# Byte classes modulo 256 of weights and rows in a two-layer hybrid block on one Trainium2 core

## What is computed

```python
a_b, a_c, a_u, q, k, v, r_g, r_u, d_v, d_g, gl = _split_cols(h @ w_in)
ys = (_short_conv(a_b, a_c, a_u, conv_a) @ w_a_out, y_b @ w_b_out,
      (jax.nn.gelu(r_g) * rec) @ w_c_out,
      _conformer_conv(d_v, d_g, conv_d, conv_d_b, ln_d_g, ln_d_b) @ w_d_out)
out = _merge(gl, ys, w_out)                      # sum of sigmoid gates times ys, @ w_out
x = x + gt1 * o
x = x + gt2 * _swiglu(_modulate(x, g_ffn[l], sh2, sc2), w_ffn_in[l], w_ffn_out[l])
```

## Time and profile before

| | |
|---|---|
| median of 3 runs | 1960.27 us (1960.24 to 1960.73) |
| the profiled execution | 1960.5 us |
| its span, first to last instruction | 1958.7 us |
| mean granted TensorE clock | 0.997 |
| TensorE busy | 1930.0 us, 11006 matmuls |
| VectorE, ScalarE, GpSimd busy | 1416.5, 908.0, 812.0 us |
| bytes read from HBM | 273.70 MB |

### The profile page before, as it was taken

One profiled execution on the slowest core, in us unless ns is written; L12 is line 12 of the kernel. 1 busy time (PEld: TensorE's weight loads), 2 busy tenths in 40 slices (PEclk: granted clock), 3 DMA queues, 4 the chain that ended last, 5 costly groups with the idle time before them and its releaser, 6 DMA issues.

```text
span 1958.7 us, 29316 instructions
## 1 busy us (share of the span) xinstructions
PE 1930.0 (99%) x11006; PEld 1671.1 (85%) x11006; DVE 1416.5 (72%) x2475; ACT 908.0 (46%) x1439; POOL 812.0 (41%) x353
## 2 busy tenths in 40 slices
PE   7999999999999999999999999999999999999998
PEld 5778888888888888887888888878899999999998
DVE  5896666677789868798885544689788787645455
ACT  5787544232223343345222223599854435565443
POOL 1002322344444444344344444301647886454432
PEclk9999999999999999999999999999999999999999
DMA  8222211222232235534455442322334554544543
GB/s 344 86 86 81 92 65 65 85 88 107 86 105 88 100 138 216 192 129 170 174 219 192 190 175 83 140 78 106 130 108 151 180 186 174 193 172 172 194 174 127
DMA packets 38701, 276.25 MB, mean 141 GB/s; under 512 B 4416, under 2 KB 4416, under 8 KB 6336
## 3 DMA queue, kind: packets, MB, share of 16 engines
q1 hardware_dynamic: 38592, 274.77, 38.2%
HBM read 273.70 MB, written 1.05 MB: 140 GB/s over the span
## 4 chain that ended last, share of the span: by engine, by line
PE 81%; DVE 13%; ACT 3%; issue 2%; DMA 0%; POOL 0%; SPq 0%; DVEq 0%; ACTq 0%; POOLq 0%
PE PS L592 80%; DVE PS L1545 3%; DVE TMP L1542 1%; DVE TMP L1545 1%; ACT WH L1023 1%; DVE TMP L1548 1%; PE PS L905 1%; DVE S L1545 1%; ACT PS L1023 1%; DVE PS L1542 1%; DVE SM L1991 1%; DVE HL L1545 0%; DVE TMP L1864 0%; DVE ZL L1542 0%; DVE WL L1542 0%
## 5 line engine op out<-in xcount | busy, mean ns | idle before, releaser
L535 POOL TENSOR_TENSOR WL<-RAW,WH 128x1024 fp32r<-128x1024 f32 (+1 forms) x337 | 802.8, 2400 | 1122.9 <-ACT WH L1023 1122.9
L1023 ACT ACTIVATE WH<-RAW 128x1024 fp32r<-128x1024 f32 (+1 forms) x416 | 414.4, 1043 | 606.0 <-PE PS L592 571.4
L592 PE MATMUL PS<-HH,WH 128*128 128x512 f32 (+2 forms) x1968 | 680.7, 346 | 7.3 <-POOL WL L535 3.2
L592 PE MATMUL PS<-HH,WL 128*128 128x512 f32 (+2 forms) x1968 | 667.5, 339 | 0.0
L592 PE MATMUL PS<-HL,WH 128*128 128x512 f32 (+2 forms) x1968 | 666.9, 340 | 0.3 <-DVE HL L1545 0.3
L592 PE MATMUL PS<-ZH,WH 128*128 128x512 f32 (+1 forms) x1312 | 442.1, 337 | 3.7 <-DVE HL L1542 2.9
L592 PE MATMUL PS<-ZH,WL 128*128 128x512 f32 (+1 forms) x1312 | 441.0, 336 | 0.0
L592 PE MATMUL PS<-ZL,WH 128*128 128x512 f32 (+1 forms) x1312 | 439.3, 337 | 0.3 <-POOL ZL L559 0.3
L592 PEld LDWEIGHTS PS<-HH,WH 128*128 128x128 f32 x1968 | 373.0, 190 | 55.8 <-issue 8.2
L592 PEld LDWEIGHTS PS<-HL,WH 128*128 128x128 f32 x1968 | 372.6, 190 | 44.0 <-issue 3.8
L592 PEld LDWEIGHTS PS<-HH,WL 128*128 128x128 f32 x1968 | 373.0, 190 | 41.3
(11 more groups left out here) (210 smaller groups left out, 1740.3 us busy)
## 6 DMA issues: line engine op xcount, KB each, us to landing
RAW<-in_stream SPq DMA_DIRECT2D x200, 1024.0 KB, 4.8
CD<-in_modw SPq DMA_DIRECT2D x22, 1024.0 KB, 7.1
G<-in_modw SPq DMA_DIRECT2D x22, 1024.0 KB, 6.9
RAW<-in_stream SPq DMA_DIRECT2D x8, 768.0 KB, 4.2
CD<-in_lruw SPq DMA_DIRECT2D x2, 2048.0 KB, 11.7
X<-in_xT SPq DMA_DIRECT2D x2, 1024.0 KB, 7.1
S<-in_modw SPq DMA_DIRECT2D x2, 1024.0 KB, 12.9
RAW<-in_modw SPq DMA_DIRECT2D x1, 1024.0 KB, 19.8
```

The source lines that it names most:

```text
L535: nc.gpsimd.tensor_tensor(WL[:, a:b], RAW[:, a:b], WH[:, a:b].bitcast(F32), ALU.subtract)\
L592: return nc.tensor.matmul(out, lhs, rhs, start=start, stop=stop)
L1023: return nc.scalar.activation(out, in_, f, **kw)
```

## The change

The second slot of WH, WL and RAW begins 32 words (128 bytes) later than the end of the first slab, by a new constant SLOT that replaces SLAB as the step between slots wherever these tensors are indexed (loads, splits, products, the home of one slab of the modulation's weights). The tensors change their order, with one 128-byte tensor in each gap, so that WH, WL, HH and HL begin at 0 modulo 256 in their first slot, the second slots of WH and WL at 128, and ZH and ZL at 128. RAW's first slot is at 128 and its second at 0. S and CD stay at 128, TMP and G go from 128 to 0, PADA from 0 to 128. All the tensors up to SM end 384 bytes later.

```diff
+SLOT = SLAB + 32
...
         MOD = sb("MOD", 2 * 48)
         X = sb("X", KC * NT)
-        WH = sb("WH", 2 * SLAB, F32R)
-        WL = sb("WL", 2 * SLAB, F32R)
+        WH = sb("WH", SLOT + SLAB, F32R)
+        SELB = sb("SELB", 32)
+        WL = sb("WL", SLOT + SLAB, F32R)
+        AMP = sb("AMP", 2 * 2 * KC)
+        HH = sb("HH", KC * UROW, F32R)
+        LC = sb("LC", 2 * 16)
+        HL = sb("HL", KC * UROW, F32R)
         ZH = sb("ZH", KC * NT, F32R)
         ZL = sb("ZL", KC * NT, F32R)
-        HH = sb("HH", KC * UROW, F32R)
-        AMP = sb("AMP", 2 * 2 * KC)
-        SELB = sb("SELB", 32)
-        LC = sb("LC", 2 * 16)
-        HL = sb("HL", KC * UROW, F32R)
         S, SR = sb_and_rounded("S", KC * NT)
         CD = sb("CD", KC * NT)
-        RAW = sb("RAW", 2 * SLAB)
+        RAW = sb("RAW", SLOT + SLAB)
...
-                a, b = s * SLAB + h * half, s * SLAB + (h + 1) * half
+                a, b = s * SLOT + h * half, s * SLOT + (h + 1) * half
...
-                a = s * SLAB + k * 2 * P + t * P
+                a = s * SLOT + k * 2 * P + t * P
...
-                        w0 = SLAB + k * 2 * P
+                        w0 = SLOT + k * 2 * P
```

More of the change, by code:

```diff
@@ L316, in build @@
         MOD_HOMES = [S[:, 0:SLAB], S[:, SLAB:2 * SLAB], CD[:, 0:SLAB], CD[:, SLAB:2 * SLAB],
-                     RAW[:, SLAB:2 * SLAB], TMP[:, 2 * NT:6 * NT], G[:, 0:SLAB], G[:, SLAB:2 * SLAB]]
+                     RAW[:, SLOT:SLOT + SLAB], TMP[:, 2 * NT:6 * NT], G[:, 0:SLAB], G[:, SLAB:2 * SLAB]]
         MOD_ORDER = [j + h * (MOD_FIRST // 2) for j in range(MOD_FIRST // 2) for h in range(2)]
@@ L459, in load @@
             def load(n, s, words=SLAB):
-                sp.dma_start(RAW[:, s * SLAB:s * SLAB + words], slab_of(stream, n)[:, 0:words]).then_inc(raw_loaded[s], 16)
+                sp.dma_start(RAW[:, s * SLOT:s * SLOT + words], slab_of(stream, n)[:, 0:words]).then_inc(raw_loaded[s], 16)
             def load_unit(w):
@@ L1028, in high @@
                 for h in halves:
-                    x = slice(s * SLAB + h * half, s * SLAB + (h + 1) * half)
+                    x = slice(s * SLOT + h * half, s * SLOT + (h + 1) * half)
                     fn(WH[:, x], RAW[:, x], ACT.Copy).then_inc(hi_done[s], 1)
@@ L1632, in low @@
                 dve.wait_ge(hi_done[s], 2 * m + 2)
-                x = slice(s * SLAB + half, s * SLAB + 2 * half)
+                x = slice(s * SLOT + half, s * SLOT + 2 * half)
                 tt(WL[:, x], RAW[:, x], WH[:, x].bitcast(F32), SUB).then_inc(lo_done[1][s], 1)
@@ L1810, in lows @@
                         dve.wait_ge(hi_done[s], 2 * m + (h + 1))
-                        x = slice(s * SLAB + h * HALF, s * SLAB + (h + 1) * HALF)
+                        x = slice(s * SLOT + h * HALF, s * SLOT + (h + 1) * HALF)
                         tt(WL[:, x], RAW[:, x], WH[:, x].bitcast(F32), SUB).then_inc(lo_done[h][s], 1)
```

## The result

The changed kernel takes 1969.79 us, the median of five runs (1967.66 to 1971.89), beside 1960.27 for the kernel before in five (1960.15 to 1960.73). The ratio is 1.0048, 95% interval 1.0035 to 1.006: slower by about 9.5 us. The profiled execution of the changed kernel is the shortest of its five, 1967.66 us with a span of 1965.9, so the two traces differ by 7.2 us.

The account below looks back on a forecast made before the run. TensorE's distance between matmul starts was taken to bound the kernel. The profiled 1960.5 us plus 3.6 for class changes, other terms 0, made 1964.1, less 0.2 to the median: 1963.9, say 1964; range 1951 to 1984.

Parts of the forecast that it names:

- What bounds the kernel: Whole kernel: TensorE, busy 1930.0 of 1958.7 us, so the distance between its matmuls' starts sets the time.
- DVE, ScalarE, GpSimd and the loads at nothing: Other engines and loads into RAW: moved starts cost 0; DVE at most 2.5 us either way.
- The price of unlike classes at 512 columns: 512-column matmuls with rows and weights in different 128-byte halves modulo 256: step stays 227 ns, 0 us; range +21 to -4.
- the rival that unlike pairs of 512 columns never settle: Unlike 512-column pairs: step 231 for 227 ns throughout, 11 us more, 1971; at the slowest steps 1981; chance 0.27.
- the bound of 8.3 ns: 512-column unlike pairs: slowest two steps after the gates, 235 ns each, +8.3 ns x 2472 = +21 us for the range.
- The price of a change of class: Layer 0, where rows' or weights' class flips between or inside slabs: 120 x 0.03 = +3.6 us; layer 1: 0.
- 256 columns at zero: 256-column unlike matmuls, mostly in layer 1: step unchanged at 120 ns, cost 0; range -3 to +5 us.
- the lower bound, -1, from the 258-column slab: 256-column matmuls: that slab's eight took 0.95 us, 119 ns each, so at best -1 ns x 2472, -3 us.
- The counts: Unlike matmuls over all stages: 2472 of 512 columns and 2472 of 256, together 4944, about half of all.
- The rival that unlike classes free the 10 ns: Every unlike pair loses 10 ns over plain fp32: 49 us less, 1911; in one length only 25, 1935; chance 0.17.
- The rival that nothing reads the layout: Whole kernel: address classes have no effect, so the time stays at 1960 us; chance 0.13.

Follow-up runs that it names:

- the kernel with 112 bytes: Kernel before with only layer 1's rows of HH, HL, ZH, ZL starting 112 bytes later: 1944.29 us, ratio 0.992.
- the sweep: Only load, rounding and groups of 52 rounded matmuls, rows' start stepped past fixed weights (another kernel steps the weights): 113.3 ns at 112 bytes, 256 columns.

## Why the prediction was right in its number and wrong in its mechanism

The forecast was 1964 us and 0.2% more; measured are 1969.79 and 0.48% more, inside the range of 1951 to 1984, and slower, to which the largest chance was given. The +3.6 us of the forecast came from a term that measured near nothing, and the +14 us that were there came from one put at nothing, so that the forecast lay near at all is luck. Step by step:

- **What bounds the kernel** held: only TensorE's steps moved, and the time followed them, less 3.5 us, of which 1.5 are a stretch of half clock that only the kernel before spent on long matmuls, and 2.0 shorter waits.
- **DVE, ScalarE, GpSimd and the loads at nothing** held: 2423 for 2421 ns, 747 for 746. The weights' whole round, though, which a faster TensorE meets, was not priced.
- **The price of unlike classes at 512 columns** is the step that failed. "I take 227 unchanged, since the 256-column pair is the nearest row and it settled": it was carried from one length to the other, and the step measured 232.4, and 233.4 in the branch stages, +5.7 to +6.7 ns. By 2472 that is +14 to +17 us, against the +13.7 + 0.6 that the traces show. This is the rival that unlike pairs of 512 columns never settle, priced at 4.4 ns and 1971 us; it had 0.27. Its evidence was in the prediction (the 258-column slab that doesn't settle), but the bound of 8.3 ns was used for the range only.
- **The price of a change of class** failed as well: 120 disturbances of 0.03 us were to be +3.6. An alike slab after an unlike one has one or two disturbed steps and is 226.8 for 226.7 on average, 0.01 to 0.02 us. What the earlier trace rows shows is real, but it was the wrong term: the cost is inside the unlike slabs, not at their edges.
- **256 columns at zero** was wrong by -1.3 ns. Four PADAR pairs at 0.01 us of resolution could not show a cycle of five with a mean of 118.7; the lower bound, -1, from the 258-column slab was nearly right. It gave back 3.6 us.
- **The counts** held: 2472 unlike pairs of each length reproduce the sum within 1 us at 512 and at 256 columns, 2472 x -1.3 = -3.2 for -3.6.
- **The rival that unlike classes free the 10 ns** was wrong for 512 columns and true in kind for 256: with the rows 112 bytes on, though not 128, half of the 13.3 ns over the columns go (113.3 for 120.0, 106.7 being the columns). The Trainium skill (TensorE: Matmul & The Clock Gate, Back-to-back issue gap) has 2.5 ns over the columns for an isolated warm matmul; the streams of rounded matmuls here don't reach it, since no settled group came under 6.6 (113.3 less 106.7).
- **The rival that nothing reads the layout** is refuted. The Trainium skill (SBUF — State Buffer, SBUF: two separate sides) describes two independent read ports for TensorE. In the runs with matmuls alone, the step goes from 226.7 to as much as 240.0 ns with nothing changed but the start of the rows. Here the two reads are not independent of each other in time, whether or not it is at these ports.

Why the second reads disturb the first isn't shown. The traces show that a weight load starts with the matmul before it: at 541.27 the matmul of HH and the load for HL both start, so the rows stream while the next weights are read. The slab's edges fit this in part: the last step of an alike slab of a_cu, whose rows are unlike the coming slab's weights, already takes 232 or 233 ns; but so does the last of an unlike slab, whose rows are alike with what is loaded. Most of the scatter from run to run goes with the granted clock: the kernel with 112 bytes took 1942.59 and 1942.81 us at 0.997, 1944.29 at 0.996, 1946.55 and 1947.31 at 0.994. Why the changed kernel scattered by 4.2 us with 0.996 in all its five runs is open.

## What to carry to other kernels

Rounded fp32 matmuls back to back have a step that depends on where the rows start relative to the weights loaded meanwhile, for starts at multiples of 32 bytes mostly modulo 256, and the sign depends on the length: at 512 columns keep them equal (226.7 ns; elsewhere up to 240), at 256 columns let the rows start 112 bytes further on (113.3 for 120.0 in the sweep and in the whole layer; weights 112 bytes on gave 120.0, and 192 bytes gave 113.3 in only half of the tiles). Such an offset costs nothing but a few bytes, so measure it per length, with whole slabs and not with a few matmuls, and don't carry a price from one length to another. When TensorE's step falls, look at the next slowest round at once: here 6% less per matmul of layer 1 was 26 us by the steps and brought 16, since the weights' round of 11.0 to 11.3 us took over.

## What the runs showed of the hardware that was not expected

- The step of a sequence is a repeating cycle, not noise: seven steps with a mean of 232.4, two of 238 and 229, five of 118.7, three of 113, 113, 114. Many of the means lie near multiples of 3.3 ns: 226.7, 230.0, 233.3, 240.0, and 113.3, 116.7, 120.0; others, 228.9 and 232.4 among them, don't.
- The 13.3 ns over the columns at equal starts isn't a floor. With other starts the 256-column step was 113.3, while no 512-column group of these runs was under 226.7.
- One distance can have more than one cycle. At 128 bytes 256 columns step by 120.0 in one kernel and 118.7 in two others, and 512 columns in the changed kernel by 232.4 in a_cu and by 233.6, once settled, in the branch stages; at 192 bytes tiles of one layer have 113.3 or 117.8. What decides between them isn't shown.
- At 512 columns some unequal starts cost nothing either: weights 240 bytes on are at 226.7, as are 120, 132 and 156 bytes.
